# Expert up products in four output tiles of 32 columns instead of two of 64

## The reference, cut to what matters

```python
h = jax.nn.silu(jnp.einsum('td,edf->tef', t, w1)) * jnp.einsum('td,edf->tef', t, w3)
h = h * gate[:, :, None].astype(h.dtype)
y = jnp.einsum('tef,efd->td', h, w2)
```

## Time and profile before

| | us |
|---|---|
| median of 2 runs (1421.18 and 1421.82) | 1421.5 |
| the profiled execution's own time | 1421.71 |
| its span, first to last instruction | 1420.0 |
| TensorE matmul rows busy | 1358.4 (96%) |
| TensorE weight loads busy | 767.6 (54%) |
| VectorE busy | 533.2 (38%) |
| ScalarE busy | 345.1 (24%) |

### The profile page before, as it was taken

The page is one execution under the profiler, slowest core; times in us unless marked ns, Lnnn a source line. Parts: engine busy times, 40 slices in busy tenths (PEclk is TensorE's granted clock), DMA queues, the critical chain, the costliest instruction groups (busy, mean ns, idle before and its releaser), DMA issues.

```text
span 1420.0 us, 19054 instructions
## 1 busy us (share of the span) xinstructions
PE 1358.4 (96%) x7250; PEld 767.6 (54%) x7250; DVE 533.2 (38%) x1013; ACT 345.1 (24%) x619; POOL 228.8 (16%) x205
## 2 busy tenths in 40 slices
PE   8999999999998999998998998999999999898987
PEld 7874898987785345434433533544544543443533
DVE  6999320544426242232312323323323322331314
ACT  1121378566571110110211111111111120111012
POOL 2002656687880000000000000000000000000000
PEclk9999999999999999999999999999999999999999
DMA  8533543434475999999999999959999999999993
GB/s 214 177 119 120 206 178 119 162 135 171 138 284 237 400 428 428 427 427 427 429 428 428 428 429 428 428 228 429 428 428 428 428 428 428 428 428 427 428 427 125
DMA packets 71541, 471.76 MB, mean 332 GB/s; under 512 B 17330, under 2 KB 17411, under 8 KB 46275
## 3 DMA queue, kind: packets, MB, share of 16 engines
q1 hardware_dynamic: 70834, 469.75, 80.7%
q10 hardware_dynamic: 528, 1.05, 0.2%
q0 software_dynamic: 128, 0.26, 0.1%
HBM read 468.95 MB, written 2.10 MB: 332 GB/s over the span
## 4 chain that ended last, share of the span: by engine, by line
PE 64%; DMA 18%; DVE 2%; ACT 1%; issue 1%; POOL 1%; DVEq 0%; POOLq 0%; ACTq 0%
PE ps L1909 25%; DMA ring<-in_expert_w_dram 18%; PE ps L1927 12%; PE ps L1567 11%; PE ps L1887 5%; PE ps L1917 3%; PE ps L1945 2%; PE ps L1946 1%; POOL w_lo L567 1%; PE ps L1899 1%; PE ps L2049 0%; PE ps L1834 0%; DVE reg_x L1495 0%; DVE reg_y L1126 0%; PE ps L1859 0%
## 5 line engine op out<-in xcount | busy, mean ns | idle before, releaser
L1927 PE MATMUL ps<-ring,reg_y 128*64 128x512 f32 x1056 | 239.1, 606 | 9.7 <-DVE reg_y L1393 6.8
L567 POOL TENSOR_TENSOR w_lo<-ring,w_hi 128x512 fp32r<-128x512 f32 x152 | 199.9, 1347 | 72.4 <-ACT w_hi L629 71.2
L1399 DVE TENSOR_TENSOR y_lo_t<-ps,y_hi_t 64x512 fp32r<-64x512 f32 x132 | 90.9, 688 | 175.0 <-ACT y_hi_t L863 172.9
L1927 PEld LDWEIGHTS ps<-ring,reg_y 128*64 128x64 f32 x1056 | 76.0, 139 | 146.2 <-issue 142.0
L863 ACT ACTIVATE y_hi_t<-ps 64x512 fp32r<-64x512 f32 x132 | 78.0, 591 | 279.7 <-PE ps L1927 278.1
L1407 DVE TENSOR_TENSOR reg_x<-ps,reg_x 128x512 f32<-128x512 f32 x128 | 82.2, 684 | 155.5 <-PE ps L1946 155.5
L1909 PE MATMUL ps<-reg_e,reg_s 128*64 128x512 f32 x528 | 119.4, 594 | 10.3 <-POOLq L592 10.3
L1909 PE MATMUL ps<-ring,reg_s 128*64 128x512 f32 x528 | 120.0, 596 | 6.8 <-POOLq L592 6.2
L1388 DVE TENSOR_SCALAR reg_y<-ps,lamv 128x512 f32<-128x512 f32 x33 | 24.8, 751 | 267.6 <-PE ps L1909 267.6
L1909 PE MATMUL ps<-ring,reg_y 128*64 128x512 f32 x528 | 120.0, 596 | 5.5 <-POOLq L592 5.0
L1909 PE MATMUL ps<-reg_e,reg_y 128*64 128x512 f32 x528 | 119.5, 595 | 3.4 <-POOLq L592 3.0
(11 more groups left out here) (402 smaller groups left out, 1759.8 us busy)
## 6 DMA issues: line engine op xcount, KB each, us to landing
ring<-in_expert_w_dram SPq DMA_DIRECT2D x128, 2048.0 KB, 20.3
reg_e<-in_expert_w_dram SPq DMA_DIRECT2D x64, 2048.0 KB, 20.4
ring<-in_w_in_dram SPq DMA_DIRECT2D x19, 2048.0 KB, 8.0
ring<-in_w_out_dram SPq DMA_DIRECT2D x8, 2048.0 KB, 7.9
reg_x<-in_x_dram SPq DMA_DIRECT2D x4, 1024.0 KB, 8.6
ring<-in_w_in_dram SPq DMA_DIRECT2D x2, 1024.0 KB, 7.3
out_dram<-reg_x SPq DMA_DIRECT2D x3, 512.0 KB, 2.7
reg_e<-in_ssm_w_glu_dram ACTq DMA_DIRECT2D x1, 1024.0 KB, 9.0
```

Source lines behind the costliest of these rows:

```text
L567: G.tensor_tensor(w_lo[:, i % BUFS, :], unit(u % SLOTS_A)[:, c, :], w_hi[:, i % BUFS, :], ALU.subtract).then_inc(row_lo, 1)
L1399: V.tensor_tensor(y_lo_t[64 * q:64 * q + 64, w], psb[3 + k // 2][64 * (k % 2):64 * (k % 2) + 64, :], y_hi_t[64 * q:64 * q + 64, w], ALU.su ...
L1927: last = M(psb[3 + i // 2][64 * (i % 2):64 * (i % 2) + 64, :], hT[:, 2 * half + f, :], unit2(s)[:, f, 512 * i:512 * i + 512], start=half = ...
```

## The change

Each product of 64 token columns becomes two products of 32 columns, `i` = 0 and 1, with the same moving operand. Chunk c goes to partitions 64 (c % 2) + 32 i. So two neighbouring chunks times two halves of the slots fill four tiles of 32 columns. The PSUM contents afterwards are the same numbers in the same places; DMAs, semaphore counts, buffers and all other engines' instructions stay as they are.

```diff
                     s = landed(n_, 2 * m + half)
                     for c in range(8):
                         cc = 8 * half + c
-                        i = c % 2
-                        last = M(psb[m][64 * i:64 * i + 64, :], xeT[half][:, c, 64 * q:64 * q + 64], unit(s)[:, c, :],
-                                 start=cc < 2, stop=cc >= DC - 2)
+                        for i in range(2):
+                            o, w = 64 * (c % 2) + 32 * i, 64 * q + 32 * i
+                            last = M(psb[m][o:o + 32, :], xeT[half][:, c, w:w + 32], unit(s)[:, c, :],
+                                     start=cc < 2, stop=cc >= DC - 2)
                     last.then_inc(slot_free, 1)
```

## The result

The changed kernel takes 1450.71 us (median of 2 runs, 1448.8 to 1452.62) against 1421.5 us: a ratio of 1.0199, 95% interval 1.0181 to 1.0217. It is slower by 29 us, which is 1.99%: clear of noise, and whether it is over 2% these runs don't settle. The forecast was 1422.2 us with a range up to 1440, so it was wrong.

The account below looks back on a forecast made before the run. DMA transfers bound 454–921 and 1160–1320 us, TensorE the extra item and tail; both were full from 945 to 1160. Products 0, shape changes 0.5, code 0: 1421.7 + 0 + 0.5 + 0 = 1422.2 us, range 1419 to 1440.

Parts of the forecast that it names:

- The products: Matmuls of `up`: all four 32-column tiles stream at once, 0.86 us per two chunks as before, cost 0.
- Issue and weight loads: Added `up` instructions: 34 ns a pair against 107 allowed, loads at most 0.28 us under a 0.43 us step; cost 0.
- Changes of shape: Tile-shape change where `up` follows `down` or `gates`: 0.16 us each, 33 in all, 0.5 us on the path.
- a rival: Four at once, not at full pace, in `up`: 1456 us at 15% slower; chance 0.10.
- Code in the hardware loop: TensorE's loop over groups grows from some 1160 to 1672 matrix instructions; bounds 0 and 2.5 us, 0 taken.
- the branch: Case that the loop over groups is not resident and code is fetched again: 1425 us, chance 0.32.
- The stall: Missing code at each of five jumps back: 3.18 us priced from the end, together 16 us, nearly all hidden.
- a lost clock: Clock rival: lowered TensorE clock after a 1 us wait, 1.7 us on the path, inside the range; no separate chance.
- the queue's lead: Transfers issued ahead, taken to cover added TensorE work from 945 us unless an issue comes late; 1.0 us cover at 1022.20.
- The upper bound of 2.5 us: Eviction cost at the jump between 1004 and 1022 us: 3.2 + 0.3 - 1.0 = 2.5 us.
- Two tiles at a time: Rival in every `up`: only two tiles stream, 454 us more TensorE work, 1841 us; chance 0.10.
- The loop's eviction: Loop over groups not staying resident, shown by instruction packets between 660 and 1230 us; 1425 us, chance 0.32.

Follow-up runs that it names:

- the shifted kernel: Changed kernel with 128 instructions more ahead of the hardware loop, from products split in two in the written-out group 0; 1423.95 us, ratio 1.0008.
- the shift runs: Changed kernel with 128 or 192 instructions more ahead of the hardware loop, none in it: 1423.95 us and 1446.19 us.
- the kernel before, written out: Kernel before the change with TensorE's hardware loop over groups 1 to 6 written out, no jump back; 1427.63 us, ratio 1.0033.
- the half change: Four tiles of 32 columns only for w1, two of 64 for w3, against the kernel before; 1425.38 us, ratio 1.002.
- three quarters of the change: Four tiles for three of an item's four halves, two of 64 for the second half of w3, against the kernel before; 1424.28 us, ratio 1.0008.

## Why the prediction was wrong

**The products.** Right. Four tiles stream at once, four starts within 80 ns, 3.43 us a half; cost 0. The reading of rows 5 and 6 carried over: matmuls of different tiles don't start strictly in program order here. One reading under a rival was wrong: 0.43 us are the step of 512 columns in one tile (L1589) and of 2 x 512 in two, not of 2 x 512 "in one tile or in two".

**Issue and weight loads.** Right at 0.

**Changes of shape.** 0.16 us forecast, 0.13 measured; the share on the path is below what the shifted kernel can show (-0.03 to +0.2%).

**Code in the hardware loop.** This step failed, in four places.

- The choice. I took 0 "because the trace shows no loop that doesn't fit". It was the term with the least behind it. I had counted that the loop would touch 8 blocks, and still gave the branch 0.32. The Trainium skill (Runtime: NRT & Kernel Launch, "Instruction fetch mechanics") gives TensorE room for 2048 instructions in blocks of 256, which is 8 blocks. The trace agrees with the block size (16 KB a packet, about 256 instructions apart), but by the shift runs a loop on 7 blocks stays and one on 8 doesn't, so that the room alone would have let this loop in.
- The stall. 3.18 us a jump, from the end of the kernel before; measured 5.14 to 5.72. That the earlier one was partly covered by the `down` in flight is argued.
- What follows a stall. I priced a lost clock at 1.7 us and as a rival of its own, "one such more or less". It comes with every stall: the gather takes 9.7 us instead of 7.7. A jump costs 5.4 + 2.0 = 7.4 us of TensorE time: a pass of the changed kernel takes 119.6 us, one of the shifted kernel 112.2 (1011.53 to 1123.74). Both have one `down` of 8.78 us, so the difference is the jump.
- What hides it. I set 3.2 us against 5.7 us of idle time a group and found it covered but for one jump. 7.4 us are not covered by 5.7; and from 945 to 1160 us, where rows 1 show 2.0 us of idle time, there are two jumps, at 1009 and at 1120 us, both exposed with their 7.4 us. The pass between them is 9.6 us longer; the other 2.2 are a clock lost in a `down`, which comes and goes with no jump near it (the shifted kernel has it in this pass, the kernel before doesn't), and the changes of shape. I let "the queue's lead" cover the second. The upper bound of 2.5 us should have been, with the measured 7.4: some 2 us for each of three jumps beyond what idle time takes, 2 x 7.4 after 945 us, and one more wait for code in the tail, 5: 26 us, worked out afterwards. The `down` at a lowered clock in that pass and small amounts are the rest.

**The rivals.** Two tiles at a time and a reduced pace did not occur. The loop's eviction stood inside the forecast, with a chance of 0.32 and a price of 2.5 us; the changed kernel and the same kernel shifted by 128 lie 27 us apart. A range that took it in at that price would have held the result.

## What to carry to other kernels

Splitting an instruction was free here on the array and not in the code. Before an edit adds instructions to a hardware loop of TensorE, count its instructions and its place: here loops on up to 7 blocks of 256 (an estimate from the times of the packets) ran from what was kept, and the three on 8 paid for every jump back, in the changed kernel 7.4 us of TensorE time. Instruction packets inside the loop's time in the DMA rows, and idle time with releaser "issue" on the first line of the body, are the sign; moving the loop's start by 128 instructions took the loss away. Idle time hides a new cost only in the stretch where it lies, and only together with what the stall does to the clock.

## What the runs showed of the hardware

- Eviction is a cliff. 64 instructions outside the loop change the time from 1424 to 1446 us.
- In a missing loop every whole pass fetches 9 packets (43 or 44 between 660 and 1230 us, four whole passes and most of a fifth), though 1730 instructions touch 8 blocks by the estimate.
- Code without jumps isn't free beside a full DMA queue: the kernel before, written out, is 0.33% slower (0.2 to 0.45%) with 22 packets more. Why stays open. So does the 0.2% (0.1 to 0.29%) of the half change, whose loop was resident; three quarters of the change show 0.08%.
- A first matmul in another tile starts past twelve instructions of other tiles: four matmuls in different column tiles start within 80 ns, with two loads and two matmuls for each product.
